# Scaling rows inside the transposing product: a diagonal matrix in place of pre-scaled rows and an identity transpose

## The chip, the cores and the metric

The kernel runs on one core of one Trainium2 chip. The metric is the device time of one launch in microseconds, as the median over several runs. Weights are streamed from HBM, all activations stay on the chip.

## The reference

The reference is a small hybrid transformer on 256 tokens of `x` and 256 tokens of context, width 1024, float32. It has an even layer (RWKV7 recurrence and window attention), a wide squared-ReLU feed-forward block, an odd layer (neighbourhood attention and global attention), a second feed-forward block, a third layer (sparse attention and retention) and a gated feed-forward block, and a last norm. What the change touches is the root-mean-square norm in front of every block:

```python
def rms_norm(x, g):
    xf = x.astype(jnp.float32)
    y = xf * lax.rsqrt(jnp.mean(xf * xf, axis=-1, keepdims=True) + NORM_EPS)
    return (y * g.astype(jnp.float32)).astype(x.dtype)

def modulate(h, gain, shift, scale):
    return rms_norm(h, gain) * (1 + scale) + shift
```

## The kernel before

The residual stream `H` lies token-major: tile k holds 128 tokens on the partitions and 1024 features in a row. The projections want the features on the partitions, so the norm of a tile k also turns it. The norm of a tile is the generator `normed(T, k)`, which puts these steps into one common `plan`; each engine then walks the plan in order and issues its own part of each step.

1. `residual` (where there is one): ScalarE takes a root (L2525), VectorE inverts it (L1931) and adds the scaled output of the block before to `H` (L1961).
2. `square`: ScalarE sums the squares of the row (L2514) and takes the root (L2516).
3. `scale rows`: VectorE inverts the root (L1931) and writes features 0 to 511 of the row times the inverse into the buffer `XH` (L1936); ScalarE does features 512 to 1023 (L2520), after it has waited for the inverse.
4. `x`, twice (q = 0 and q = 4): TensorE turns four 128x128 blocks of the scaled rows into one PSUM bank with `transpose` (L1477). The q = 0 wait is for VectorE's half, the q = 4 wait for ScalarE's half. VectorE applies gain and shift to the q = 0 bank (four instructions, L1948, or L1950 where there is no shift), ScalarE to the q = 4 bank (four instructions, L2538).
5. `x hi`: ScalarE rounds both halves to the fp32r type (L2473). `x lo`: VectorE subtracts to get the rest (L1955). The projections (L1412 to L1414) multiply such pairs in three products and wait for `x lo`.

There are 18 such tile norms: four each before the even layer (T = m0), the first feed-forward block (f0) and the odd layer (m1), two each before the second feed-forward block (f1), the third layer (m2) and the last feed-forward block (u). For f0, m1, f1 and m2 the steps are woven into the output projection that comes before: of the tiles of that projection, tile m is finished (L2551 squares it on ScalarE, L1972, L1975 or L1978 gate it on VectorE), and then the norm of tile m starts; the `x` step of a tile comes between or behind later products of the projection in TensorE's order. In f1 and m2 the order on ScalarE is: L2551 of tile 1, gain and shift of tile 0 (L2538), root for the residual of tile 1 (L2525), rounding of tile 0, squares of tile 1. In m0 and u the tiles follow each other without a projection between them.

`spread` makes a row vector into a 128x1024 tile: the vector stands on the partitions, is read as a broadcast 128x128 block, and is turned by TensorE (L1485), four blocks for each half; ScalarE copies out the first half, VectorE the second (L1926). There are 8 spreads, 64 transposed blocks: two for each of two gates, one for each of two more gates, one for the retention norm and one for the last norm.

Operands of the transposes and of these products are float32. `split_product` of the large projections works on fp32r views instead.

Of the kernel before, what the change touches and what calls it, by code (L numbers as in the profile page):

```python
def program(nc, I, C, out):
# [8 lines left out]
    ACT = mybir.ActivationFunctionType  # L10
    AX = mybir.AxisListType
    MUL, ADD, SUB, MAX = ALU.mult, ALU.add, ALU.subtract, ALU.max
# [9 lines left out]
    extra = ctx.enter_context(nc.sbuf_tensor("extra", [128, 3584], F32))  # L22
# [73 lines left out]
    pe, ve, sc, gp, sp = Line("tensor_done"), Line("vector_done"), Line("scalar_done"), Line("pool_done"), Line("sync_done")  # L96
    ENG = [pe, ve, sc, gp]
    table = {}

    def at(*key):  # L100
        return table.setdefault(key, Point())
# [16 lines left out]
    def sb(*shape):  # L118
        n = 1
        for x in shape:  # L120
            n *= x
        a = arena[:, top[0]:top[0] + n]
        top[0] += n
        assert top[0] <= AREA, top[0]
        if len(shape) == 2:
            a = a.rearrange("p (a b) -> p a b", a=shape[0])
        elif len(shape) == 3:
            a = a.rearrange("p (a b c) -> p a b c", a=shape[0], b=shape[1])
        return a
# [29 lines left out]
    XT, XH = sb(8, 512), sb(8, 512)  # L159
# [8 lines left out]
    H = sb(4, 1024)  # L168
# [4 lines left out]
    DER = sb(8, 8, 2)  # L173
    SSQ = sb(4, 2)
    RS = sb(4, 4)
    SV = sb(8, 32)
    arow = [sb(256), sb(256)]
    sel = sb(2)
# [2 lines left out]
    ident = sb(128)  # L181
# [7 lines left out]
    def step(*a):  # L189
        plan.append(a)  # L190
# [10 lines left out]
    def take(*key):  # L201
        assert idle, "no bank"
        b, before = idle.pop(0)
        assert key not in uses, key
        uses[key] = Use(b, before)

    def give(*key):
        u = uses[key]
        idle.append((u.b, u.empty))

    def bank(*key):
        return uses[key]
# [148 lines left out]
    def col(name, j=0, n=1):  # L361
        r = place[name][0]
        return VC[:, r + j:r + j + n]
# [27 lines left out]
    norms = {}  # L391
# [7 lines left out]
    def normed(T, k, before=None):  # L399
        if before:  # L400
            step("residual", T, k)
        yield
        step("square", T, k)
        yield
        step("scale rows", T, k)
        yield
        for q in (0, 4):
            take("x", T, k, q)
            step("x", T, k, q)
            give("x", T, k, q)  # L410
        yield
        for q in (0, 4):
            step("x hi", T, k, q)
        yield
        for q in (0, 4):
            step("x lo", T, k, q)
        yield

    def rows_of(k, q):
        return H[:, k, q * 128:q * 128 + 512].rearrange("p (a b) -> p a b", a=4)  # L420

    def scaled_rows(k, q):

        return XH[:, q:q + 4, k * 128:k * 128 + 128]

    def x_ready(T, ks):
        return [at("x lo", T, k, 4) for k in ks]
# [88 lines left out]
    step("root table")  # L516
    norms["m0"] = Norm(*at_x(0), None, [at("h", 0)], [at("gain", 0)])
    tiles = [normed("m0", k) for k in range(4)]
    step("load h", 0)
    for n, _ in enumerate(modulation(0, 0, 8)):  # L520
# [402 lines left out]
    def others():  # L923
        for k in FIRST[:7]:
# [11 lines left out]
    norms["f0"] = Norm(*ff_x(0, 1), "mix0", [at("h", 1), *stage("recurrence")], [at("gain", 1)])  # L936
    out_proj("mix0", [(I["w_out"][0], k, k, 4) for k in (4, 0)], OP, 4, O_e, (), {k: [at("part o", k)] for k in range(8)}, gate=True,
             then=[normed("f0", k, True) for k in range(4)])
    xr = x_ready("f0", range(4))
    step("end", "mix0")  # L940
# [7 lines left out]
    def ffn(i, ntok, xr, T, norm_gain, norm_shift, points):  # L948
# [8 lines left out]
        for part in range(32 // nt):  # L957
# [30 lines left out]
            if end:  # L988
                norms[T] = Norm(norm_gain, norm_shift, ("ff2", i, part), [*stage(("ff1", i, part))])
            out_proj(("ff2", i, part), parts, F.h1, ntok, F.O, (), {j: [at("ff1 part", i, part, j)] for j in range(nt)},  # L990
                     part > 0, end, then=[normed(T, k, True) for k in range(ntok)] if end else ())
        return x_ready(T, range(ntok))

# [221 lines left out]
    for pair in range(4):  # L1215
        g = pair // 2
        for qt in range(2):
            q, n = qN[:, pair, qt * 128:qt * 128 + 128], 128 * (qt + 1)
# [188 lines left out]
    def tensor(e):  # L1407
# [50 lines left out]
        def mod(i, s):  # L1458
            w, u = chunks["mod", i, s], bank("mod", i, s)
            pe.wait_ge(w.landed, u.before, at("sv"))  # L1460
            for k in range(8):
                q = 32 * (k % 4)
                t = e.matmul(u.b[q:q + 32, 0:256], SV[:, k, :], w.v[:, k, :], start=k < 4, stop=k >= 4)  # L1463
            t.then_inc(*pe.tick(u.full, w.used))
# [7 lines left out]

        def norm_x(T, k, q):
            u = bank("x", T, k, q)
            pe.wait_ge(at("scaled rows", T, k, q), u.before)
            for j in range(4):
                t = e.transpose(u.b[:, j * 128:j * 128 + 128], scaled_rows(k, q)[:, j, :], ident)  # L1477
            t.then_inc(*pe.tick(u.full))

        def spread(key, half):  # L1480
            vecs, dst, points = spreads[key]
            u = bank("spread", key, half)
            pe.wait_ge(u.before, *points)
            for j in range(4):
                t = e.transpose(u.b[:, j * 128:j * 128 + 128], vecs(half * 4 + j).to_broadcast([128, 128]), ident)  # L1485
            t.then_inc(*pe.tick(u.full))

        def wide(w, x, x0, m, u, first, stop, *points, last=False):
# [391 lines left out]
    def vector(e):  # L1880
        ve.begin(e)

        def vc(part):
            u = bank("vc", part)
            ve.wait_ge(ve.last(), u.full)
            if part == 0:
                e.tensor_copy(VC[:, 0:128], u.b[:, 0:128]).then_inc(*ve.tick(u.empty, at("vc 0")))
                ve.wait_ge(ve.last())
                e.memset(SV, 0.0).then_inc(*ve.tick(at("sv zero")))
                e.memset(eps, 1e-6).then_inc(*ve.tick())  # L1890
                e.memset(eps_gn, 64e-5).then_inc(*ve.tick(at("eps")))
            else:
                e.tensor_copy(VC[:, 128:row], u.b[:, 128:row]).then_inc(*ve.tick(u.empty, at("vc 1")))
# [34 lines left out]
        def inverse(k, *rooted):  # L1928

            ve.wait_ge(ve.last(), at(*rooted))  # L1930
            e.reciprocal(RS[:, k, 2:3], RS[:, k, 1:2]).then_inc(*ve.tick(at("inv", *rooted)))  # L1931

        def scale_rows(T, k):
            inverse(k, "root", T, k)
            ve.wait_ge(ve.last(), *norms[T].points)
            e.tensor_scalar(scaled_rows(k, 0), rows_of(k, 0), RS[:, k, 2:3], None, MUL).then_inc(*ve.tick(at("scaled rows", T, k, 0)))  # L1936

        def norm_x(T, k, q):
            p, u, s = norms[T], bank("x", T, k, q), 0 if k < 2 else 1
# [17 lines left out]
        def residual(T, k):  # L1957
            p = norms[T]
            inverse(k, "res root", T, k)
            ve.wait_ge(ve.last(), *p.points)  # L1960
            e.scalar_tensor_tensor(out=H[:, k, :], in0=outs[p.of].O[:, k, :], scalar=RS[:, k, 2:3], in1=H[:, k, :], op0=MUL,  # L1961
                                   op1=ADD).then_inc(*ve.tick(at("residual", T, k)))

        def out_block(name, c, m):
            p, u, s = outs[name], bank("out", name, c, m), slice(c * 512, c * 512 + 512)
            o, i, r = p.O[:, m, s], u.b[:, :], GB[:, m // 2, s]
            if p.gate and c:
                ve.wait_ge(ve.last(), at("out square", name, 0, m))
                e.tensor_scalar(RS[:, m, 3:4], SSQ[:, m, 0:1], 1.0 / 1024, 1e-6, MUL, ADD).then_inc(*ve.tick(at("first squares", name, m)))
            if p.add:  # L1970
# [466 lines left out]
        def final(k):  # L2437
# [7 lines left out]
                *ve.tick(at("final", k)))  # L2445

        steps = {"vc 0": lambda: vc(0), "vc 1": lambda: vc(1), "turn": turn, "split": split, "gain": gain, "gate": gate,
                 "spread": spread, "scale rows": scale_rows, "x": norm_x, "x lo": x_lo, "residual": residual, "out block": out_block,
                 "even start": even_start, "qB": qB_, "vB": vB_, "sink": sink, "pA": pA_, "rotate": rotate_, "swap": swap_,
                 "round masks": round_masks, "round caus": round_caus, "scores": scores, "scale p": scale_p, "values": values, "recurrence start": recurrence_start,  # L2450
                 "unit grams": unit_grams, "unit tlt": unit_tlt,
# [16 lines left out]
    def scalar(e):  # L2468
# [20 lines left out]
        def silu():  # L2489
            sc.wait_ge(sc.last(), at("vc 0"), at("sv zero"))  # L2490
            e.activation(SV[:, :, 0], col("c", 0, 8), ACT.Silu).then_inc(*sc.tick())
            sc.wait_ge(sc.last())
            e.activation(SV[:, :, 1], col("c_ctx", 0, 8), ACT.Silu).then_inc(*sc.tick(at("sv")))

# [16 lines left out]
        def square(T, k):  # L2511
            p = norms[T]
            sc.wait_ge(sc.last(), *([at("residual", T, k)] if p.of else []), *p.points)
            e.activation(JUNK, H[:, k, :], ACT.Square, accum_out=RS[:, k, 0:1]).then_inc(*sc.tick(at("squared", T, k)))  # L2514
            sc.wait_ge(sc.last(), at("eps"))
            e.activation(RS[:, k, 1:2], RS[:, k, 0:1], ACT.Sqrt, scale=1.0 / 1024, bias=eps).then_inc(*sc.tick(at("root", T, k)))  # L2516

        def scale_rows(T, k):
            sc.wait_ge(sc.last(), at("inv", "root", T, k), *norms[T].points)
            e.activation(scaled_rows(k, 4), rows_of(k, 4), ACT.Identity, scale=RS[:, k, 2:3]).then_inc(*sc.tick(at("scaled rows", T, k, 4)))  # L2520

        def residual(T, k):
            p = norms[T]
# [312 lines left out]
        def final(k):  # L2836
# [4 lines left out]
            e.activation(tiny[:, 4 * k + 1:4 * k + 2], a, ACT.Sqrt, scale=1.0 / 1024, bias=eps).then_inc(*sc.tick(at("final root", k)))  # L2841

        steps = {"load h": load_h, "more columns": more_columns, "silu": silu, "mod": mod, "split": split, "spread": spread,
                 "square": square, "root table": root_table, "scale rows": scale_rows, "x": norm_x, "x hi": x_hi,
                 "residual": residual, "out block": out_block,
                 "even start": even_start, "kB": kB_, "vB": vB_, "pA": pA_, "pA gates": pA_gates, "scores": scores, "turn p": turn_p,
                 "unit grams": unit_grams, "unit lt": unit_lt, "unit turned": unit_turned, "unit lv": unit_lv, "unit solve": unit_solve,
# [125 lines left out]
    block = ctx.enter_context(nc.Block())  # L2973
# [107 lines left out]
```

## Time and profile before

| | us |
|---|---|
| median of 3 runs | 2058.72 (2058.27 to 2063.38) |
| the profiled execution | 2063.38 |
| its span, first to last instruction | 2061.6 |
| TensorE matmul busy | 1844.8 (89%) |
| TensorE weight load busy | 1537.0 (75%) |
| VectorE busy | 1100.0 (53%) |
| ScalarE busy | 904.6 (44%) |
| GpSimd busy | 216.2 (10%) |

The mean granted TensorE clock is 0.943 of full speed. Most of the time TensorE is fed without a gap; where blocks meet, it waits for VectorE and ScalarE. The profiled execution was the slowest of the three runs shown.

### The profile page before, as it was taken

The numbers are of one execution on the slowest core, as the hardware profiler recorded it, in microseconds if no ns is written. First come the engines' busy times: TensorE is split into PE (matmuls) and PEld (weight loads), VectorE is DVE, ScalarE is ACT, GpSimd is POOL, SyncE is SP. The second block draws the span as 40 slices with busy tenths as digits, with TensorE's granted clock in tenths as the row PEclk, the third lists the DMA queues.
The fourth block names the chain that finished last, engine by engine and source line by source line (L and its number), as shares of the span: only waits on it lengthen the run. The fifth ranks groups of instructions, "written<-read, shape, count | busy, mean of one in ns | idle before, by whom it ended". The sixth has DMA issues, their size and how long they took to land.

```text
span 2061.6 us, 39782 instructions
## 1 busy us (share of the span) xinstructions
PE 1844.8 (89%) x16802; PEld 1537.0 (75%) x16802; DVE 1100.0 (53%) x1671; ACT 904.6 (44%) x1448; POOL 216.2 (10%) x214
## 2 busy tenths in 40 slices
PE   5899879899888889999996999799979999679997
PEld 3777658778777778888886776698877677569985
DVE  1457565465555554324435766565445674556863
ACT  3326545344332353223325356565342465346652
POOL 0000034425253000000000200010000000000210
PEclk9999889999998989999998999899989999789998
DMA  8332233222231222333233420355544434245543
GB/s 272 94 123 90 91 112 105 85 84 84 84 105 64 82 82 82 102 102 93 91 102 72 124 81 28 107 182 187 192 131 155 152 103 139 72 132 164 184 156 110
DMA packets 201375, 237.16 MB, mean 115 GB/s; under 512 B 14347, under 2 KB 158573, under 8 KB 201197
## 3 DMA queue, kind: packets, MB, share of 16 engines
q1 hardware_dynamic: 195856, 227.33, 34.7%
q10 hardware_dynamic: 5341, 7.30, 1.0%
q8 instruction: 132, 2.16, 0.4%
q14 instruction: 46, 0.38, 0.1%
HBM read 233.56 MB, written 1.05 MB: 114 GB/s over the span
## 4 chain that ended last, share of the span: by engine, by line
PE 75%; DVE 11%; ACT 7%; issue 2%; POOL 2%; DMA 1%; SPq 1%; ACTq 1%; DVEq 0%; POOLq 0%
PE bank L1412 18%; PE bank L1413 17%; PE bank L1414 17%; PE bank L1604 9%; ACT window L2473 2%; DVE window L1906 2%; PE bank L1592 2%; PE bank L1571 2%; PE bank L1583 2%; PE bank L1463 1%; PE bank L1611 1%; SPq L2934 1%; PE bank L1789 1%; ACT arena L2538 1%; PE bank L1575 1%
## 5 line engine op out<-in xcount | busy, mean ns | idle before, releaser
L1412 PE MATMUL bank<-window 128*128 128x512 f32 (+1 forms) x2152 | 768.6, 357 | 64.8 <-DVE window L1955 27.8
L1413 PE MATMUL bank<-window 128*128 128x512 f32 (+1 forms) x2152 | 754.1, 350 | 0.0
L1414 PE MATMUL bank<-window 128*128 128x512 f32 (+1 forms) x2152 | 753.8, 350 | 0.0
L1412 PEld LDWEIGHTS bank<-window 128*128 128x128 f32 x2152 | 419.6, 195 | 131.1 <-DVE window L1906 32.4
L1906 DVE TENSOR_TENSOR window<-arena,window 128x2048 fp32r<-128x2048 f32 (+1 forms) x164 | 371.4, 2265 | 272.3 <-ACT window L2473 270.4
L2473 ACT ACTIVATE window<-arena 128x2048 fp32r<-128x2048 f32 (+3 forms) x292 | 377.1, 1291 | 198.3 <-PE bank L1414 121.4
L1414 PEld LDWEIGHTS bank<-window 128*128 128x128 f32 x2152 | 419.0, 195 | 50.9
L1413 PEld LDWEIGHTS bank<-window 128*128 128x128 f32 x2152 | 420.2, 195 | 48.1 <-issue 0.2
L2473 ACT ACTIVATE arena<-bank 128x256 f32<-128x256 f32 (+1 forms) x298 | 127.0, 426 | 370.7 <-PE bank L1414 134.9
L1604 PE MATMUL bank<-arena 64*64 64x64 f32 (+1 forms) x5888 | 218.1, 230 | 18.9 <-DVE arena L1398 10.5
L1604 PEld LDWEIGHTS bank<-arena 64*64 64x64 f32 x5888 | 204.8, 139 | 35.4 <-DVE arena L1398 12.2
L2880 POOL TENSOR_TENSOR arena<-arena 128x256 f32<-128x256 f32 x80 | 67.8, 848 | 409.1 <-ACT arena L2473 303.1
L2695 ACT ACTIVATE arena<-bank 128x512 f32<-128x512 f32 (+1 forms) x64 | 31.4, 491 | 142.0 <-PE bank L1414 140.7
L2108 DVE TENSOR_TENSOR arena<-arena,bank 128x512 f32<-128x512 f32 (+1 forms) x80 | 50.7, 634 | 64.7 <-PE bank L1604 63.7
L2597 ACT ACTIVATE arena<-bank,arena 128x512 f32<-128x512 f32 (+3 forms) x112 | 58.5, 522 | 55.0 <-DVE arena L2052 34.0
L2241 DVE TENSOR_TENSOR arena<-arena 128x512 f32<-128x512 f32 (+1 forms) x48 | 29.0, 603 | 78.8 <-ACT arena L2695 78.3
L1463 PE MATMUL bank<-arena 128*32 128x256 f32 x768 | 58.3, 426 | 13.3 <-DMA arena<-in_w_ada 13.1
L2052 DVE TENSOR_REDUCE arena<-bank 128x1 f32<-128x512 f32 (+4 forms) x96 | 51.7, 538 | 22.9 <-PE bank L1575 17.0
L2902 POOL TENSOR_TENSOR arena<-arena 128x2048 f32<-128x2048 f32 x2 | 11.1, 5560 | 483.1 <-DMA arena<-in_c_rpb 483.1
L2473 ACT ACTIVATE extra<-bank 128x512 f32<-128x512 f32 (+2 forms) x96 | 46.9, 489 | 19.4 <-PE bank L1583 16.8
L1470 PEld LDWEIGHTS bank<-arena 128*128 128x128 f32 x192 | 29.0, 213 | 25.5 <-ACT arena L2473 12.1
L1477 PE MATMUL bank<-arena 128*128 128x128 f32 x144 | 26.2, 347 | 23.8 <-DVE arena L1936 23.3
(286 smaller groups left out, 1668.1 us busy)
## 6 DMA issues: line engine op xcount, KB each, us to landing
arena<-in_w_ff SPq DMA_DIRECT2D x64, 1024.0 KB, 5.3
arena<-in_w_ada SPq DMA_DIRECT2D x48, 1024.0 KB, 5.7
arena<-in_w_in SPq DMA_DIRECT2D x23, 1024.0 KB, 5.1
arena<-in_w_ffn_up SPq DMA_DIRECT2D x22, 1024.0 KB, 5.1
arena<-in_w_ffn_down SPq DMA_DIRECT2D x10, 1024.0 KB, 5.1
arena<-in_w_in_even SPq DMA_DIRECT2D x9, 1024.0 KB, 5.5
arena<-in_w_out SPq DMA_DIRECT2D x8, 1024.0 KB, 5.1
arena<-in_w_in_odd SPq DMA_DIRECT2D x8, 1024.0 KB, 5.3
```

The source lines that it names most:

```text
L1412: e.matmul(o, rr(l[0]), rr(r[0]), start=start, stop=False)
L1413: e.matmul(o, rr(l[0]), rr(r[1]), start=False, stop=False)
L1414: return e.matmul(o, rr(l[1]), rr(r[0]), start=False, stop=stop)
L1463: t = e.matmul(u.b[q:q + 32, 0:256], SV[:, k, :], w.v[:, k, :], start=k < 4, stop=k >= 4)
L1571: t = e.matmul(b if it["ns"] > 1 else b[:, 0], it["q"][h0:h1], k, start=True, stop=not it["masks"])
L1604: t = e.matmul(o[h0:h1, c], l[i][h0:h1, c], r[i][h0:h1, c], start=i == 0, stop=i == len(l) - 1)
L1906: e.tensor_tensor(rr(raw), raw, rr(w.high, F32), SUB).then_inc(*ve.tick(w.ready))
L2052: e.tensor_reduce(low[:, h * ns:h * ns + ns], b, AX.X, MAX, negate=True).then_inc(*ve.tick(at("max", S, i, h)))
L2108: e.tensor_tensor(w, w, x, SUB).then_inc(*ve.tick(b.empty, at("w", *u)))
L2473: return e.activation(o, i, ACT.Copy, **k)
L2597: e.activation(a.P[i % a.NP][h][:, s * n:s * n + n], u.b[:, s * n:s * n + n], ACT.Exp, bias=low[:, x:x + 1], accum_out=total[:, x:x + 1]). ...
L2880: return e.tensor_tensor(z.L[l % 2], z.G[:, :, 0], lvl[:, 1 - d, l:l + 1, :].to_broadcast([128, NCH, 64]), MUL)
```

## The change

The step `scale rows` becomes a step `diag`: VectorE inverts the root as before and then writes the identity matrix times the inverse, a 128x128 diagonal matrix, into a part of the buffer `extra` that nothing else uses in those stretches. ScalarE has no part in it. TensorE's `x` step multiplies each 128x128 block of the raw `H` with that diagonal matrix by a plain `matmul` in float32 in place of `transpose`; scale and turn come out of one product. Both halves wait only for `diag`. In `spread` the call `transpose` becomes a plain `matmul` with the identity.

```diff
+    DIAG = extra[:, 2048:2560].rearrange("p (a b) -> p a b", a=4)
...
-        step("scale rows", T, k)
+        step("diag", T, k)
...
-    def rows_of(k, q):
-        return H[:, k, q * 128:q * 128 + 512].rearrange("p (a b) -> p a b", a=4)
-
-    def scaled_rows(k, q):
-
-        return XH[:, q:q + 4, k * 128:k * 128 + 128]
...
         def norm_x(T, k, q):
             u = bank("x", T, k, q)
-            pe.wait_ge(at("scaled rows", T, k, q), u.before)
+            pe.wait_ge(at("diag", T, k), u.before)
             for j in range(4):
-                t = e.transpose(u.b[:, j * 128:j * 128 + 128], scaled_rows(k, q)[:, j, :], ident)
+                t = e.matmul(u.b[:, j * 128:j * 128 + 128], H[:, k, (q + j) * 128:(q + j) * 128 + 128], DIAG[:, k, :],
+                             start=True, stop=True)
             t.then_inc(*pe.tick(u.full))
...
             for j in range(4):
-                t = e.transpose(u.b[:, j * 128:j * 128 + 128], vecs(half * 4 + j).to_broadcast([128, 128]), ident)
+                t = e.matmul(u.b[:, j * 128:j * 128 + 128], vecs(half * 4 + j).to_broadcast([128, 128]), ident, start=True, stop=True)
...
-        def scale_rows(T, k):
+        def diag(T, k):
             inverse(k, "root", T, k)
             ve.wait_ge(ve.last(), *norms[T].points)
-            e.tensor_scalar(scaled_rows(k, 0), rows_of(k, 0), RS[:, k, 2:3], None, MUL).then_inc(*ve.tick(at("scaled rows", T, k, 0)))
+            e.tensor_scalar(DIAG[:, k, :], ident, RS[:, k, 2:3], None, MUL).then_inc(*ve.tick(at("diag", T, k)))
...
-        def scale_rows(T, k):
-            sc.wait_ge(sc.last(), at("inv", "root", T, k), *norms[T].points)
-            e.activation(scaled_rows(k, 4), rows_of(k, 4), ACT.Identity, scale=RS[:, k, 2:3]).then_inc(*sc.tick(at("scaled rows", T, k, 4)))
```

## Rows read from the trace of the kernel before

**Rows 1.** The page, part 4: shares of the chain that ended last.
```profile
PE 75%; DVE 11%; ACT 7%; issue 2%; POOL 2%; DMA 1%; SPq 1%; ACTq 1%; DVEq 0%; POOLq 0%
```

**Rows 2.** Groups by shape, TensorE: shapes xcount | busy us, mean ns | idle before.
```profile
L1470 PE MATMUL bank<-arena 128*128 128x2 f32 x192 | 31.8, 270 | 10.4 <-ACT arena L2473 10.4
L1477 PE MATMUL bank<-arena 128*128 128x128 f32 x144 | 26.2, 347 | 23.8 <-DVE arena L1936 23.3 <-ACT arena L2520 0.4
```

**Rows 3.** Timeline, TensorE: start us, us from first start to last end.
```profile
1747.41 0.38 PE L1823 MATMUL bank<-arena 128*128 128x128 f32 x2
...
767.40 1.91 PE L1485 MATMUL bank<-arena 128*128 128x128 f32 x16
```

**Rows 4.** Single lines: min/median/max ns, first to last start; the last row is the timeline's.
```profile
L1485 PE MATMUL bank<-arena x64: 270/272/473, 650.8 to 2048.6; 128*128 128x128 f32 x64
...
L1936 DVE TENSOR_SCALAR arena<-arena x18: 485/486/490, 33.6 to 1844.7; 128x512 f32<-128x512 f32 x18
L2520 ACT ACTIVATE arena<-arena x18: 721/722/727, 37.9 to 1845.2; 128x512 f32<-128x512 f32 x18
...
1086.36 0.15 DVE L1969 TENSOR_SCALAR arena<-arena 128x1 f32<-128x1 f32 x1
```

**Rows 5.** Timeline of f0, ScalarE, VectorE and TensorE.
```profile
719.79 0.73 ACT L2520 ACTIVATE arena<-arena 128x512 f32<-128x512 f32 x1 [0.36 <-DVE arena L1931]
720.55 1.44 ACT L2538 ACTIVATE arena<-bank,arena 128x128 f32<-128x128 f32 x3
...
722.52 1.30 ACT L2473 ACTIVATE window<-arena 128x512 fp32r<-128x512 f32 x2
...
720.25 1.75 DVE L1948 TENSOR_SCALAR arena<-bank,arena 128x128 f32<-128x128 f32 x4
...
740.04 0.72 ACT L2520 ACTIVATE arena<-arena 128x512 f32<-128x512 f32 x1 [0.36 <-DVE arena L1931]
...
750.45 1.06 PE L1477 MATMUL bank<-arena 128*128 128x128 f32 x8
```

**Rows 6.** Timeline of m1, ScalarE, norm of tile 3.
```profile
1115.75 0.72 ACT L2520 ACTIVATE arena<-arena 128x512 f32<-128x512 f32 x1 [0.36 <-DVE arena L1931]
```

**Rows 7.** Timeline of f1, TensorE, ScalarE and VectorE.
```profile
1302.55 1.09 PE L1477 MATMUL bank<-arena 128*128 128x128 f32 x8
1310.01 1.97 PE L1477 MATMUL bank<-arena 128*128 128x128 f32 x8 [6.37 <-DVE arena L1936]
...
1302.82 0.60 ACT L2551 ACTIVATE extra<-bank 128x512 f32<-128x512 f32 x1
...
1303.74 1.93 ACT L2538 ACTIVATE arena<-bank,arena 128x128 f32<-128x128 f32 x4 [0.23 <-PE bank L1477]
...
1306.12 0.16 DVE L1931 RECIPROCAL arena<-arena 128x1 f32<-128x1 f32 x1
```

**Rows 8.** Timeline of m2, ScalarE.
```profile
1501.17 1.57 ACT L2538 ACTIVATE arena<-bank,arena 128x128 f32<-128x128 f32 x4 [0.24 <-PE bank L1477]
```

**Rows 9.** Timeline of u, TensorE and ScalarE.
```profile
1845.17 2.82 PE L1477 MATMUL bank<-arena 128*128 128x128 f32 x12 [0.36 <-ACT arena L2520]
...
1846.39 3.27 ACT L2538 ACTIVATE arena<-bank,arena 128x128 f32<-128x128 f32 x8 [0.51 <-PE bank L1477]
```

**Rows 10.** Timeline of m0, all engines.
```profile
48.99 6.21 PE L1477 MATMUL bank<-arena 128*128 128x128 f32 x32
...
50.99 3.89 ACT L2538 ACTIVATE arena<-bank,arena 128x128 f32<-128x128 f32 x8 [3.56 <-PE bank L1477]
...
60.68 0.58 PE L1412 MATMUL bank<-window 128*128 128x256 f32 x1 [5.48 <-DVE window L1955]
```

**Rows 11.** Windows of f1: length, busy of PE, PEld, DVE, ACT, POOL; granted clock; DMA.
```profile
1316.00:1318.00 2.00, 1.75 (x8) 1.76 (x9) 0.99 (x3) 1.27 (x1) 0.00 (x0) 0.50 0.00 0
...
1320.00:1322.00 2.00, 2.00 (x17) 2.00 (x16) 0.18 (x1) 0.38 (x1) 0.00 (x0) 0.87 0.00 0
```

**Rows 12.** The chain in order of time, a spread inside the recurrence.
```profile
665.18 1.04 PE bank L1485 x4
```

More of the change, by code:

```diff
@@ L2447, in vector @@
         steps = {"vc 0": lambda: vc(0), "vc 1": lambda: vc(1), "turn": turn, "split": split, "gain": gain, "gate": gate,
-                 "spread": spread, "scale rows": scale_rows, "x": norm_x, "x lo": x_lo, "residual": residual, "out block": out_block,
+                 "spread": spread, "diag": diag, "x": norm_x, "x lo": x_lo, "residual": residual, "out block": out_block,
                  "even start": even_start, "qB": qB_, "vB": vB_, "sink": sink, "pA": pA_, "rotate": rotate_, "swap": swap_,
@@ L2843, in scalar @@
         steps = {"load h": load_h, "more columns": more_columns, "silu": silu, "mod": mod, "split": split, "spread": spread,
-                 "square": square, "root table": root_table, "scale rows": scale_rows, "x": norm_x, "x hi": x_hi,
+                 "square": square, "root table": root_table, "x": norm_x, "x hi": x_hi,
                  "residual": residual, "out block": out_block,
```

## The prediction

> **What bounds the kernel.** I read the chain that ended last first. TensorE holds three quarters of it, VectorE and ScalarE together 18% [rows 1]: long runs of products, and joints where a norm runs on VectorE and ScalarE. The edit sits at the joints, so I took the groups by shape for the counts, then the chain and the timeline of each engine around all six norms. What the reader should see is that work of the norm is on the path in some places (a row of TensorE that waits for L1936) and beside other work elsewhere.
>
> **Price of the new product.** The 96 plain float32 products of the modulation turn (48 turns, two each) are 192 records; the 144 transposes of the norms (18 tiles of eight) are 144 records, and those of the spreads (eight of eight) are 64 [rows 2, 4]. So a plain float32 product is issued as two load and multiply records, a transpose as one. Sixteen transposes take 1.91 us; less the length of one (0.27) that is 1.64/15 = 0.11 us apiece. A plain product of the same shape, L1823, takes 0.38 for its two records, and again (0.38 - 0.27) = 0.11 lies between them [rows 3, 4]. Hence one extra record of 0.11 us for each of the 208 blocks at full clock. At half clock eight transposes take 1.97, (1.97 - 0.42 - small gaps)/7 = 0.213 apiece [rows 7]. One tile costs 0.88 us more on TensorE at full clock and 1.7 at half clock, a half spread 0.44 or 0.85.
>
> The Trainium skill, page "TensorE: Matmul & The Clock Gate", section Terms, has a transpose mode that is four times faster for FP32. By that each block would gain three records' time and not one; the rows of L1823 speak for one. I keep it as a rival.
>
> **Price of what goes.** VectorE's 128x512 multiply takes 0.486 us, ScalarE's 0.722 [rows 4]. The new 128x128 multiply does not stand in the trace: it is bounded by 0.15 (one column) and 0.486 (512 columns) [rows 4]; a line between them gives 0.15 + 0.336/4 = 0.23, so VectorE saves 0.25 a tile (0 to 0.34). ScalarE saves its 0.72 and the 0.36 for which it stood waiting on the inverse.
>
> **f0.** ScalarE's L2520 at 719.79 stands in front of gain and shift of the tile before, 720.55, already turned. Without it these start at 719.45, 1.1 earlier. But rounding, at 722.52, also needs VectorE's four L1948, which end at 722.00 and come only 0.25 earlier, at 721.75; with the handover rounding starts at 721.8, so 0.7 is won and not 1.1 [rows 5]. The same happens a tile later (0.7). After the scale of the last tile, 740.04, ScalarE goes straight on to rounding a weight chunk for which TensorE waits: 1.1 won in full. TensorE's extra 0.88 for tiles 0 and 1 falls where it is some 2.7 us ahead of ScalarE, and for tile 2 in a wait; it costs nothing there. If that cover were gone it would be 0.9 each. The turn of tile 3, at 750.45, is on the chain: +0.9 [rows 5]. Sum -0.7 - 0.7 - 1.1 + 0.9 = -1.6.
>
> **m1.** The same pattern, with the last scale at 1115.75 in front of five DMA issues and a chunk's rounding, all of which move up [rows 6], and VectorE's 0.25 once more, since the gate of tile 1 follows L1936 directly: -1.9.
>
> **f1.** Here nothing is ahead. L2551 at 1302.82 can't move up: TensorE reaches the turn at 1302.55 straight out of the product that L2551 reads, whose tail ends about 1302.7. The q = 4 bank is full after 16 records instead of 8, 0.9 later; ScalarE already waits for it (0.23 idle) and starts gain and shift at 1304.6 instead of 1303.74. They end at 1306.5, and the root L2525 for the residual of tile 1 is queued behind them and ends at 1306.9, so VectorE's inverse comes at 1306.95 instead of 1306.12: +0.8. Then the residual, squares and root follow unchanged; VectorE's diagonal is 0.25 faster; TensorE's turn of tile 1 at 1310.01 is on the path at half clock: +1.7 [rows 7]. Sum +2.3.
>
> **m2.** As f1, but gain and shift take 1.57 and not 1.93 [rows 8], so the delay of the inverse is 0.7: +0.7 - 0.25 + 1.7 = +2.1.
>
> **u.** Sixteen transposes at half clock, the last twelve from 1845.17, are read by eight ScalarE instructions from 1846.39 to 1849.66 [rows 9]. New: the first diagonal is 0.25 earlier and nothing waits for ScalarE, so 32 records run from 1843.45 and end at 1843.45 + 31 x 0.213 + 0.42 = 1850.5. The second four of ScalarE start then, not at 1848.1, and end at 1852.1: +2.4 with half clock throughout. If the clock rises on the way, up to 1.0 comes back. I take +1.9.
>
> **m0.** The scales are done by 41 us, in a wait for a weight DMA: nothing is won. The 32 transposes last 6.21 us, which is 24 gaps of 0.213 and 7 of 0.11: the clock rises near 54.2. ScalarE's reading starts after eight records and runs without a gap until the projection starts at 60.68 [rows 10]. New: ScalarE's first bank is full at 48.99 + 15 x 0.213 + 0.42 = 52.6, its second at 55.2, where it would have been free at 54.7; the rest follows at its own pace. Sum +2.2 (1.5 with an earlier rise).
>
> **Spreads.** The one at 665.18 is on the chain at half clock: +0.85 [rows 12]. Sixteen records at 767.40 in the gapless run of the feed-forward block [rows 3]: +1.75. The pair before the odd gate +0.44, the one in the second feed-forward block +0.88, the last norm's +0.88. Those at 650.8 and 1739.7 lie in waits of TensorE: 0 (0.44 and 0.88 if the cover goes). Sum +4.8.
>
> No DMA, no SP or GpSimd instruction moves except the five issues in m1. No new wait is made; the q = 4 turn waits for VectorE where it waited for ScalarE.
>
> **Total.** -1.6 - 1.9 + 2.3 + 2.1 + 1.9 + 2.2 + 4.8 = +9.8 us, 0.48%. On the profiled execution, 2063.38, that gives 2073.2. That execution was 4.7 above the median, so for the median I add the same to 2058.72: 2068.5.
>
> **Rivals.**
> *The clock gives it back.* In f1 TensorE idles 6.37 us before the turn, its records there have the half-clock spacing [rows 7], and the projection that starts at 1316.25 still runs at 0.50 until about 1320.3 [rows 11]. With twice the records in the turn, the clock could be up when the projections start in m0, f1, m2 and u; with four slow starts like this one of 4 us, half of 16, 8, would come back: +2, 2060.6. For it: m0's clock did rise during the turn [rows 10]. Against: afterwards TensorE still idles about 4 us in each place, and in m0 it was down again after such a pause. The Trainium skill, the same page, Part 4: PE-mode transpose, says that transposes do not count as busy for the clock; by it plain products would help here more than m0 lets one expect. Chance 0.19.
>
> *Only the relief counts.* If the second record of a block cost nothing (the pair done inside the 0.11 of one), the place that decides is the turn itself; from under 0.03 us for an extra record the sum changes sign. Then f0 and m1 give -2.5 and -2.75, f1 and m2 -0.3 each, u -0.9, in all -6.8: 2051.9. Against it stands L1823. Chance 0.08.
>
> *Three extra records per block.* The TensorE terms of the path triple: the positive parts of f0 and m1 become 5.3, f1 and m2 5.2 + 1.6 each, u and m0 about 8 each, spreads 14.4, relief -6.8: about +43, 2101. Chance 0.05.
>
> **Numbers.** My forecast has 0.68, its own range +5 to +15 (2063.7 to 2073.7): below, if the cover is better or the clock rises earlier; above, if the two hidden spreads, tiles 0 to 2 of f0 and m1 and the cold readings of u all count (0.4 + 0.9 + 5.3 + 0.5 = 7, of which I take most). The range for 8 in 10 reaches down to the clock rival and leaves out the other two: 2059.5 to 2075.5. A measurement here tells about 0.3%, 6.2 us, from no change. Slower by more: 0.62 of my forecast's 0.68 and the last rival's 0.05, 0.67; within: the clock rival and the low end of mine, 0.25; faster 0.08.
>
> **What would show it.** L1477 with 288 records and L1485 with 128, 0.11 apart; VectorE's diagonal at about 0.23 us; ScalarE's L2520 gone and gain and shift of f0 right behind the root; in f1 and m2 a longer wait of ScalarE for the turn of tile 0, and about 3.6 us for the turn of tile 1; the projection of u starting about 11 us after the root of tile 1 instead of 9. The prediction is wrong if the extra records are not 0.11 apart, if the clock is up at the start of the projections, or if in f0 TensorE turns out not to be ahead.

## The result and the profile after

The changed kernel takes 2073.48 us in the median (2071.06 to 2074.85, 4 runs) against 2060.22 (2058.27 to 2063.38, 4 runs) for the kernel before on the same chip. The ratio of the runs is 1.0057, with a 95% interval from 1.0040 to 1.0076: 0.57% slower, about 11.7 us. The two medians themselves lie 13.3 us apart; here and below, a difference in us that stands beside a ratio is worked out from the ratio. The forecast was 0.48% slower, 9.8 us. Its time, 2068.5, was 5 us low; 1.5 of these come from before's own median, which was 2060.22 in these runs and not 2058.72. The profiled executions have spans of 2061.6 and 2070.3, 8.7 apart.

The chain that ended last, and the two groups of the norms' turn, from the page and the groups of the changed kernel (shares by engine; line, shapes xcount | busy us, mean ns | idle before):

```profile
PE 75%; DVE 11%; ACT 6%; issue 2%; POOL 2%; DMA 1%; SPq 1%; ACTq 1%; DVEq 0%; POOLq 0%
...
L1471 PE MATMUL bank<-extra,arena 128*128 128x128 f32 x288 | 43.0, 316 | 17.7 <-DVE extra L1931 17.7
L1471 PEld LDWEIGHTS bank<-extra,arena 128*128 128x128 f32 x288 | 41.7, 230 | 19.7 <-DVE extra L1931 19.2
```

Single lines of the changed kernel (min/median/max ns), the spreads' product and the new diagonal:

```profile
L1480 PE MATMUL bank<-arena x128: 270/275/580, 652.0 to 2057.3; 128*128 128x128 f32 x128
...
L1931 DVE TENSOR_SCALAR extra<-arena x18: 285/286/289, 33.9 to 1851.0; 128x128 f32<-128x128 f32 x18
```

The counts are 288 and 128 where they were 144 and 64 [rows 2, 4]: one more record per block, as forecast. TensorE's wait for VectorE before the turn went from 23.3 [rows 2] to 17.7 us. The diagonal takes 0.286 us.

Timeline of f0 in the changed kernel, to be held against [rows 5]:

```profile
718.76 1.93 ACT L2529 ACTIVATE arena<-bank,arena 128x128 f32<-128x128 f32 x4
721.20 1.30 ACT L2468 ACTIVATE window<-arena 128x512 fp32r<-128x512 f32 x2 [0.50 <-DVE arena L1943]
...
719.35 1.75 DVE L1943 TENSOR_SCALAR arena<-bank,arena 128x128 f32<-128x128 f32 x4
...
737.79 3.85 ACT L2468 ACTIVATE window<-arena 128x2048 fp32r<-128x2048 f32 x2
...
747.43 2.37 PE L1471 MATMUL bank<-extra,arena 128*128 128x128 f32 x16
```

Gain and shift on ScalarE start right behind the root, and then ScalarE waits 0.50 us for VectorE before it can round: the 1.1 us shrink to 0.6, close to the 0.7 of the prediction and for its reason.

Timeline of f1 in the changed kernel, to be held against [rows 7]:

```profile
1302.91 1.95 PE L1471 MATMUL bank<-extra,arena 128*128 128x128 f32 x16
1311.00 3.79 PE L1471 MATMUL bank<-extra,arena 128*128 128x128 f32 x16 [6.15 <-DVE extra L1931]
1319.05 0.58 PE L1406 MATMUL bank<-window 128*128 128x256 f32 x1 [4.26 <-DVE window L1950]
...
1303.16 0.60 ACT L2542 ACTIVATE extra<-bank 128x512 f32<-128x512 f32 x1 [1.29 <-PE bank L1408]
...
1304.95 1.93 ACT L2529 ACTIVATE arena<-bank,arena 128x128 f32<-128x128 f32 x4 [1.10 <-PE bank L1471]
1306.91 0.29 ACT L2516 ACTIVATE arena<-arena 128x1 f32<-128x1 f32 x1
...
1307.31 0.16 DVE L1926 RECIPROCAL arena<-arena 128x1 f32<-128x1 f32 x1 [0.88 <-ACT arena L2516]
```

The squares of tile 1's projection (L2542) now show a wait for TensorE, but start no later: 0.25 us behind the start of the turn, 0.27 before. The turn of tile 0 makes ScalarE wait 1.10 us instead of 0.23, the root L2516 queues behind gain and shift, and VectorE, which had no wait there, waits 0.88. The second turn takes 3.79 us instead of 1.97.

Windows of f1 in the changed kernel (length, busy of PE, PEld, DVE, ACT, POOL; granted clock; DMA), against [rows 11]:

```profile
1314.00:1316.00 2.00, 0.79 (x4) 0.49 (x3) 0.86 (x3) 1.05 (x3) 0.00 (x0) 0.77 0.00 0
1316.00:1318.00 2.00, 0.00 (x0) 0.00 (x0) 0.43 (x1) 1.90 (x4) 0.00 (x0) 1.00 0.00 0
1318.00:1320.00 2.00, 0.95 (x4) 0.96 (x5) 1.13 (x3) 1.97 (x2) 0.00 (x0) 0.58 0.00 0
1320.00:1322.00 2.00, 2.00 (x12) 2.00 (x11) 1.82 (x1) 0.07 (x1) 0.00 (x0) 0.50 0.00 0
...
1324.00:1326.00 2.00, 2.00 (x14) 2.00 (x14) 0.42 (x1) 0.38 (x1) 0.00 (x0) 0.71 0.00 0
```

The clock rises at the end of the turn, is up while TensorE idles, and is down again when the projection starts at 1319.05. The projection then runs slowly to about 1325.2, some 6 us, where it was 4 before.

For the other norms I take one stretch each from both traces, from the first row of squares of tile 0 (in m0 from the first turned record) to the first product of the block behind it that needs the last tile's norm (in m0 that of the projection's first half). In us:

| | before | changed | measured | forecast |
|---|---|---|---|---|
| m0 | 48.99 to 60.68 | 49.28 to 62.05 | +1.1 | +2.2 |
| f0 | 712.11 to 755.78 | 711.77 to 754.07 | -1.4 | -1.6 |
| m1 | 1084.06 to 1135.19 | 1084.20 to 1134.05 | -1.3 | -1.9 |
| f1 | 1300.23 to 1316.24 | 1300.39 to 1319.05 | +2.7 | +2.3 |
| m2 | 1497.66 to 1513.07 | 1502.18 to 1519.83 | +2.2 | +2.1 |
| u | 1841.38 to 1853.35 | 1847.69 to 1860.62 | +1.0 | +1.9 |
| sum | | | +4.3 | +5.0 |

### The profile page after: what moved, and what is told of

Same layout as the page of the kernel before. It is cut to its first block, busy times and chain, and to the rows that moved or that the text cites. A ratio compares the mean times of both kernels' runs of the same rounds, so it can differ in the third digit from the quotient of the medians.

```text
span 2070.3 us, 40165 instructions
## 1 busy us (share of the span) xinstructions
PE 1856.4 (90%) x17010; PEld 1554.2 (75%) x17010; DVE 1098.3 (53%) x1671; ACT 891.6 (43%) x1430; POOL 216.5 (10%) x214
## 4 chain that ended last, share of the span: by engine, by line
PE 75%; DVE 11%; ACT 6%; issue 2%; POOL 2%; DMA 1%; SPq 1%; ACTq 1%; DVEq 0%; POOLq 0%
PE bank L1406 18%; PE bank L1407 17%; PE bank L1408 17%; PE bank L1599 9%; ACT window L2468 2%; DVE window L1901 2%; PE bank L1587 2%; PE bank L1566 2%; PE bank L1578 2%; PE bank L1457 1%; PE bank L1471 1%; SPq L2925 1%; PE bank L1606 1%; PE bank L1784 1%; DVE window L1950 1%
## 5 line engine op out<-in xcount | busy, mean ns | idle before, releaser
L1599 PEld LDWEIGHTS bank<-arena 64*64 64x64 f32 x5888 | 201.8, 137 | 35.9 <-issue 12.2
L2893 POOL TENSOR_TENSOR arena<-arena 128x2048 f32<-128x2048 f32 x2 | 11.1, 5568 | 480.5 <-DMA arena<-in_c_rpb 480.4
L1471 PE MATMUL bank<-extra,arena 128*128 128x128 f32 x288 | 43.0, 316 | 17.7 <-DVE extra L1931 17.7
L1471 PEld LDWEIGHTS bank<-extra,arena 128*128 128x128 f32 x288 | 41.7, 230 | 19.7 <-DVE extra L1931 19.2
```

The costliest lines, as they stand in the source:

```text
L1471: t = e.matmul(u.b[:, j * 128:j * 128 + 128], H[:, k, (q + j) * 128:(q + j) * 128 + 128], DIAG[:, k, :], start=True, stop=True)
L1599: t = e.matmul(o[h0:h1, c], l[i][h0:h1, c], r[i][h0:h1, c], start=i == 0, stop=i == len(l) - 1)
```

## The experiments

Ratios are to the kernel before, whose runs on the same chip had medians of 2059.6, 2059.4 and 2062.5 us in the three groups of four.

**The spreads alone.**

```diff
-                t = e.transpose(u.b[:, j * 128:j * 128 + 128], vecs(half * 4 + j).to_broadcast([128, 128]), ident)
+                t = e.matmul(u.b[:, j * 128:j * 128 + 128], vecs(half * 4 + j).to_broadcast([128, 128]), ident, start=True, stop=True)
```

> Kernel before with only the spreads changed to plain products. Theory A (each plain 128x128 product is one record of 0.11 us more, and it counts where TensorE is on the chain): +4.8 us, ratio 1.0023. Rival B (TensorE's added records lie beside other work, and what the changed kernel lost is the moment at which the clock rises and falls): within 1 us of before, ratio 1.000. Rival C (a record costs more than 0.11 us there): over +8 us.

Measured: 1.0023 (1.0011 to 1.0036), 2064.17 us, +4.7. Theory A: B's 1.000 lies below the interval, and C's +8 us is a ratio of 1.0039, above it. Two sites can be read from the traces, by the start of the same instructions in both kernels: the changed kernel loses 1.8 us at the spread of 767 and 0.9 at that of the last norm, this kernel 1.9 and 1.0; the forecast had 1.75 and 0.88. The row of the spreads in its trace:

```profile
L1485 PE MATMUL bank<-arena x128: 270/275/580, 647.2 to 2049.0; 128*128 128x128 f32 x128
```

**The norms alone.** The changed kernel with the line above turned back.

> Changed kernel with transposes again in the spreads; norms by the diagonal product. Theory A: relief and cost of the norms sum to +5.0 us, ratio 1.0024, and this plus the spread run gives the whole change, +9.8. Rival B: the whole of the change's 11.8 us stays here, ratio 1.0057. Rival D (the relief outweighs, the spreads alone are the loss): below before, ratio 0.999 or less.

Measured: 1.0042 (1.0026 to 1.0059), 2069.84 us over 5 runs, +8.7 (5.4 to 12.2). D falls. B's 1.0057 lies inside this interval; what speaks against B is the run before, in which the spreads alone cost 4.7 us. A's 1.0024 lies just below the interval. The sum with the spreads is +13.4, and the whole change is 8.2 to 15.7, so the two parts add up within their scatter; the norms cost more than the 5.0 that the forecast gave them.

**Relief without the second record.**

```diff
-                t = e.matmul(u.b[:, j * 128:j * 128 + 128], H[:, k, (q + j) * 128:(q + j) * 128 + 128], DIAG[:, k, :],
-                             start=True, stop=True)
+                t = e.transpose(u.b[:, j * 128:j * 128 + 128], H[:, k, (q + j) * 128:(q + j) * 128 + 128], ident)
```

> As the changed kernel, with the diagonal matrix still made and waited for, but the blocks of the raw rows turned by a transpose, so that the scaling by the inverse root is left out of the result; transposes in the spreads. It has the relief of VectorE and ScalarE without the second record. Theory A: f0 -2.5, m1 -2.75, f1 and m2 -0.3 each, u -0.9, in all -6.8 us, ratio 0.9967. Rival E (ScalarE's scale was hidden, VectorE waits for TensorE anyway): within 1.5 us of before.

This kernel leaves the scale out of its result and serves for timing alone. Measured: 0.9965 (0.9951 to 0.9980), 2053.79 us, -7.2. Theory A. In its trace the norm of u, from the squares at 1830.15 to the end of the last `x lo` at 1841.24, takes 11.1 us against 11.9 before. The turn of f1 is back at its old length and ScalarE's wait at 0.26:

```profile
1294.51 1.10 PE L1471 MATMUL bank<-arena 128*128 128x128 f32 x8
1301.77 1.97 PE L1471 MATMUL bank<-arena 128*128 128x128 f32 x8 [6.16 <-DVE extra L1930]
...
1295.71 1.93 ACT L2528 ACTIVATE arena<-bank,arena 128x128 f32<-128x128 f32 x4 [0.26 <-PE bank L1471]
```

**Cost without the relief.**

```diff
-                t = e.transpose(u.b[:, j * 128:j * 128 + 128], scaled_rows(k, q)[:, j, :], ident)
+                t = e.matmul(u.b[:, j * 128:j * 128 + 128], scaled_rows(k, q)[:, j, :], ident, start=True, stop=True)
```

> Kernel before with the rows still scaled by VectorE and ScalarE, and each block of them turned by a plain product with the identity instead of a transpose; spreads as before. Theory A: the cost of the norms alone, m0 +2.2, f0 and m1 +0.9 each, f1 +2.5, m2 +2.4, u +2.6, in all about +11.5 us, ratio 1.0056. Rival B (hidden): under +3 us. With the relief run it should add up to the norm run: -6.8 and +11.5 give +4.7.

Measured: 1.0063 (1.0046 to 1.0079), 2073.97 us over 6 runs, +13.0. Theory A. With the relief's -7.2 this makes +5.8. Its f1 shows the cost with the old scaling in place:

```profile
1302.51 2.05 PE L1477 MATMUL bank<-arena 128*128 128x128 f32 x16
1310.91 3.42 PE L1477 MATMUL bank<-arena 128*128 128x128 f32 x16 [6.35 <-DVE arena L1936]
...
1304.66 1.93 ACT L2538 ACTIVATE arena<-bank,arena 128x128 f32<-128x128 f32 x4 [1.19 <-PE bank L1477]
```

**The diagonal product at some norms only.** Five kernels are the kernel before with one condition that says which tile norms go by the diagonal product; the spreads stay transposes.

```diff
+    def by_diag(T, k):
+        return T in ("f0", "m1")
...
+                if by_diag(T, k):
+                    t = e.matmul(o, H[:, k, (q + j) * 128:(q + j) * 128 + 128], DIAG[:, k, :], start=True, stop=True)
+                else:
+                    t = e.transpose(o, scaled_rows(k, q)[:, j, :], ident)
...
++            o, i = (DIAG[:, k, :], ident) if by_diag(T, k) else (scaled_rows(k, 0), rows_of(k, 0))
+            e.tensor_scalar(o, i, RS[:, k, 2:3], None, MUL).then_inc(*ve.tick(at("scaled rows", T, k, 0)))
...
+            if by_diag(T, k):
+                return
             sc.wait_ge(sc.last(), at("inv", "root", T, k), *norms[T].points)
```

> Kernel before, with the diagonal product in the eight tile norms of f0 and m1 only. Theory A (where ScalarE's scale stood in front of other work and TensorE is ahead, the change wins): the prediction's -3.5 us, ratio 0.9983; by the trace of the changed kernel, where f0 and m1 won 1.0 and 1.5, -2.5, ratio 0.9988. Rival F (the norms lose wherever they are put): above 1.001.

Measured: 0.9990 (0.9978 to 1.0001), 2057.51 us, -2.1. F's loss is excluded, and both of A's numbers lie inside; the sign is A's, though no change at all is just inside the interval. In its trace the stretches of the table take 41.4 us in f0 and 48.9 in m1, against 43.7 and 51.1.

> Kernel before, with the diagonal product in the four tile norms of f1 and m2 only. Theory A: +4.4 us by the prediction, +4.9 by the trace of the changed kernel, ratio 1.0021 to 1.0024. Rival F (the loss is spread evenly over the 18 tiles, 5.0 x 4/18): +1.1, ratio 1.0005.

Measured: 1.0026 (1.0014 to 1.0039), 2066.04 us, +5.4. Theory A; the even spread of F is below the interval. The four tiles of f1 and m2, 4 of 18, lose far more than an even share.

> Kernel before, with the diagonal product in the six tile norms of m0 and u only. Theory A at half clock throughout: +4.1 us, ratio 1.0020. If the clock rises during the longer turn, as the trace of the changed kernel shows it: +1.35 and +0.96, ratio 1.0011.

Measured: 1.0045 (1.0031 to 1.0060), 2068.65 us over 6 runs, +9.3. Neither expectation: too much by a factor of two. In its trace the norm of u, 1842.48 to 1856.61, takes 14.1 us, +2.2: half clock until the last few records. That is more than in the changed kernel's trace, but leaves some 5 us unexplained. So I ran the two halves and the pair again.

> Kernel before, with the diagonal product in the four tile norms of m0 only. m0 and u together came out at 1.0045, though in that run's trace m0 itself was 0.8 to 1.1 us longer and u 2.2. Theory A (local cost): +1.1 us, ratio 1.0005. Rival H (the later start of what follows m0 moves TensorE's clock in the recurrence and costs there): 1.002 or more, with the squares of f0 more than 3 us later than before's.

Measured: 1.0021 (1.0009 to 1.0032), 2066.57 us, +4.3. A's 1.0005 lies below the interval (1.9 to 6.6 us). H asked for 1.002 or more and for squares of f0 more than 3 us later; they start at 715.52 instead of 712.11, so both hold by number. But H's reason, the clock in the recurrence, is not shown: 2.7 of these 3.4 us are there by 100 us already, and traces of kernels that share the old m0 scatter by more (below). Here the turn took 9.75 us and not 8.63, since the clock rose later, and the projection's slow start came after it. That start lasts about 5.0 us at half clock instead of 3.7, which costs some 0.6 more on top of the 2.0 of the stretch:

```profile
49.10 9.75 PE L1483 MATMUL bank<-extra,arena 128*128 128x128 f32 x64
62.82 0.58 PE L1416 MATMUL bank<-window 128*128 128x256 f32 x1 [3.98 <-DVE window L1964]
```

> Kernel before, with the diagonal product in the two tile norms of u only. Theory A: +2.2 us at half clock, ratio 1.0011. Rival H (something behind u is hit as well): 1.002 or more.

Measured: 1.0006 (0.9989 to 1.0022), 2063.67 us, +1.2. This is nearer to A's 1.0011, but H's 1.002 lies inside the interval too; the run does not decide. The rows of u:

```profile
1835.88 6.69 PE L1483 MATMUL bank<-extra,arena 128*128 128x128 f32 x32 [3.08 <-DVE extra L1945]
1847.93 0.58 PE L1416 MATMUL bank<-window 128*128 128x256 f32 x1 [5.35 <-DVE window L1964]
```

Thirty-two records in 6.69 us, all but the last few at half clock (the clock rose near 1841.9), and the projection 14.2 us after the squares at 1833.77, +2.2.

> The kernel of the m0 and u run once more, on the same chip as its two halves. Theory A: +3.3 us, ratio 1.0016, the sum of the halves; then the 1.0045 of the first time was the scatter of the clock over six runs. Rival H: 1.0045 again.

Measured: 1.0035 (1.0021 to 1.0049), 2070.00 us, +7.2. The expected 1.0016 is excluded; the two halves add up to 1.0027, which is not. H's 1.0045 lies inside as well. Taken with the first run of this kernel, m0 and u together cost 7.2 to 9.3 us, where the forecast's terms for them are 4.1; how that is shared between m0 and u these runs do not settle.

**The same relief without the product.** ScalarE's part of the scaling is given to engines that idle at that moment.

```diff
+    def by_pool(T, k, q):
+        return T in ("f0", "m1") and (q == 4 or k != 2)
...
+        def scale_rows(T, k):
+            for q in (0, 4):
+                if by_pool(T, k, q):
+                    gp.wait_ge(gp.last(), at("inv", "root", T, k), *norms[T].points)
+                    e.tensor_scalar(scaled_rows(k, q), rows_of(k, q), RS[:, k, 2:3], None, MUL).then_inc(
+                        *gp.tick(at("scaled rows", T, k, q)))
```

> Kernel before (transposes everywhere), but in f0 and m1 GpSimd scales the second half of each row instead of ScalarE, and for tiles 0, 1 and 3 the first half instead of VectorE too. It has the relief of ScalarE and VectorE and no second record. Theory A: 1.0 for each of the two tiles that stand in front of gain and shift and 1.1 for the last, in f0 and in m1: -6.2 us, ratio 0.9970. Rival G (GpSimd's multiply is too slow, about 1.7 us a half, and TensorE waits for it in its place, or it slows VectorE): at or above 0.9995.

Measured: 0.9983 (0.9968 to 0.9997), 2055.31 us, -3.5. Faster. The interval holds A's 0.9970 and, just, G's 0.9995. By the trace f0 shortens from 43.7 to 40.4 us and m1 does not (51.4 against 51.1), so the relief is whole in one place and lost in the other. In m1 the five DMA issues behind the block's end wait for all engines, GpSimd's multiplies of tile 3 among them, and ScalarE's rounding of the chunk waits behind these issues:

```profile
1109.35 3.22 POOL L2910 TENSOR_SCALAR arena<-arena 128x512 f32<-128x512 f32 x2 [10.43 <-DVE arena L1934]
...
1112.68 0.35 ACTq L2492 DMA_DIRECT2D arena<-t_Rax  x1
...
1115.48 1.91 ACT L2478 ACTIVATE window<-arena 128x2048 fp32r<-128x2048 f32 x1 [6.56 <-issue]
```

The next version keeps GpSimd for tiles 0 to 2 and lets VectorE scale both halves of tile 3:

```diff
+        return T in ("f0", "m1") and k < 3
...
             e.tensor_scalar(scaled_rows(k, 0), rows_of(k, 0), RS[:, k, 2:3], None, MUL).then_inc(*ve.tick(at("scaled rows", T, k, 0)))
+            if T in ("f0", "m1"):
+                e.tensor_scalar(scaled_rows(k, 4), rows_of(k, 4), RS[:, k, 2:3], None, MUL).then_inc(*ve.tick(at("scaled rows", T, k, 4)))
```

> Kernel before (transposes everywhere), but in f0 and m1 GpSimd scales both halves of the rows of tiles 0 to 2, and VectorE both halves of tile 3, where VectorE is idle; so that no DMA issue waits for GpSimd. Theory A: 1.0 + 1.0 + 1.1 us in f0, the same and a little more in m1, -6.2 us, ratio 0.9970. Rival G (GpSimd's two multiplies take 3.2 us, and TensorE's turn of tile 2 comes too late): 0.999 or more.

Measured: 0.9963 (0.9946 to 0.9979), 2056.28 us, -7.6. Theory A; G's 0.999 is excluded. The kernel beats both others. In its trace f0 takes 39.5 us and m1 48.1, 4.2 and 3.1 less than before, which together is near the 7.6 of the timed runs. The issues in m1 now start 1.2 us after the root ends at 1104.37, instead of 3.8, and VectorE's two multiplies of 0.49 end at 1105.55:

```profile
1104.66 0.49 DVE L1941 TENSOR_SCALAR arena<-arena 128x512 f32<-128x512 f32 x1
1105.07 0.48 DVE L1943 TENSOR_SCALAR arena<-arena 128x512 f32<-128x512 f32 x1
...
1105.58 0.35 ACTq L2494 DMA_DIRECT2D arena<-t_Rax  x1
```

## Why the prediction was right, and where it was off

**The price of the product** held. One record more per block, 16 records in 1.95 us at full clock, (1.95 - 0.27)/15 = 0.11 apart. The rival of three extra records does not show in this kernel's rows: 288 records for 144 blocks, factor two. The Trainium skill ("TensorE: Matmul & The Clock Gate", Terms) calls transpose mode four times faster for FP32; the traces here show about twice, eight blocks in 1.04 us as transposes (at 717.32 in the trace before) and in 1.95 as products.

**The price of the diagonal** was put at 0.23 and is 0.286; the line between a one-column and a 512-column row was too low. It costs 0.05 us per tile.

**f0 and m1.** TensorE was ahead, as supposed, and the reliefs are there, a little smaller: 0.6 for each of the two tiles and not 0.7, since rounding waits for VectorE, whose diagonal is slower than forecast. Up to the `x lo` of tile 2 m1 takes 29.8 us in the changed kernel against 31.2, of which 0.2 is the earlier gate; the relief run and the norms run show the same 29.8. The end of m1 won less than forecast, and for this the rows give a cause. The five DMA issues were put 1.1 us earlier, the length of ScalarE's scale and its wait. But they wait for the end of the block on all engines, so now for VectorE's diagonal. Before:

```profile
1116.56 0.35 ACTq L2487 DMA_DIRECT2D arena<-t_Rax  x1
```

In the changed kernel:

```profile
1113.82 0.29 ACT L2511 ACTIVATE arena<-arena 128x1 f32<-128x1 f32 x1
...
1114.41 0.28 DVE L1931 TENSOR_SCALAR extra<-arena 128x128 f32<-128x128 f32 x1
...
1114.73 0.35 ACTq L2482 DMA_DIRECT2D arena<-t_Rax  x1
```

The issues start 0.6 us behind the root's end where it was 1.2, so 0.6 is won and not 1.1. With 1.4 won before and 0.8 lost at the last turn this gives the 1.3 of the table. Beyond that the stretch of m1 scatters: it takes 48.9 us in the run with f0 and m1 and 50.5 in the norms run, with the same code in it.

**f1 and m2** held to 0.4 us in the stretches of the table, and the run with these two alone gives +5.4 for the forecast 4.4. The stretches end at the first product; f1's slow start behind it is 2 us longer, which costs about 1 more, while m2's ends 3.3 us behind the first product instead of 5.4, which gives about 1 back. The wait that moved, TensorE before ScalarE before the root before VectorE's inverse, is in the rows above.

**The spreads** were +4.8 by forecast and +4.7 (2.3 to 7.4) by their own run.

**m0 and u.** For u the forecast took a value between half clock throughout and a clock that rises on the way. Both occur: 5.46 us for the 32 records in the changed kernel, 6.69 in the run with u alone. The first is the exception: five of the six traces with the plain product in u have +2.2 or +2.3 for the stretch, the changed kernel's alone +1.0. For m0 the stretch to the projection became longer by 1.1 in the changed kernel and by about 2.0 in the run with m0 alone (49.10 to 62.82, 13.7 against 11.7); there the clock rises near 54.2, as in the trace before, and the forecast 2.2 fits, while in the changed kernel it rises near 52. What the prediction did not ask is whether the shift costs something behind m0. The kernels with the old m0 start the squares of f0 between 705.7 and 717.1 us, their mean over seven traces is 709.7; the six with the plain product in m0 start between 711.8 and 718.1, mean 714.2. That is +4.5, of which the norm itself has 1 to 2. It would fit the +4.3 of m0 alone. But it is not shown that such a cost exists, nor how it would arise: among the seven that do not differ there the start scatters by 11 us, and 4.5 between means of seven and six is not far outside such scatter.

**The clock rival** (0.19) was right in that the mean granted clock rose, from 0.943 to 0.955, and wrong in what this gives. In f1 the gain lies in the turn and in the idle time behind it, and the slow start of the projection grew; m2's shrank by as much. In f0 and m1 the clock is indeed up when the first half of the projection starts (its first row takes 0.39 us at 732.02, against 0.58 at 733.96 before), but TensorE then waits for a weight chunk all the same (4.12 and 9.10 us, against 3.93 and 7.89). What the clock gave elsewhere I did not isolate. The relief rival (0.08) is refuted by L1471's own records, and the relief run measured its size: forecast -6.8, measured -7.2.

**The total.** Of the 8.7 us between the two spans the stretches of the table have 4.3, and what lies between them 4.4, next to the forecast's 4.8 for the spreads. That closeness is luck in part. By the starts and ends in the table, the changed kernel gains 1.7 us from m0 to f0, where a spread was to cost 0.85, and loses 1.9 from f0 to m1, 1.3 from m1 to f1 and 1.7 from f1 to m2. The timed runs say 11.7, with an interval that begins at 8.2, so the forecast 9.8 is inside. The term that came out too small is that of m0 and u together, 4.1 by forecast and 7.2 and 9.3 in two runs whose intervals both begin above it; its rest of some 3 us or more stays open. The parts do not close either: -2.1 for f0 and m1, +5.4 for f1 and m2 and 7.2 to 9.3 for m0 and u make 10.5 to 12.6, where the norms in one kernel cost 8.7 (5.4 to 12.2).

## What to carry to other kernels

Folding a scale into a transposing product looks like saving a pass over the rows, but in float32 it trades one record per block for two on the engine that carries three quarters of the chain. Price such an edit site by site: the same edit won 0.6 us where ScalarE's multiply stood in front of work that was ready, and lost 2.2 to 2.7 us where the turn itself was next. And where an in-order engine does something early that nobody needs yet, give it to an engine that idles there; but look which later waits ask for that engine's end.

## What the runs showed that I had not expected

The scatter of one and the same kernel goes with the clock. Of 29 runs of the kernel before in the second group of four, the fastest (2051.98 us) had a mean granted clock of 0.949 and the slowest (2068.51) one of 0.940; over all 29 the correlation of time and clock is -0.94. By these two clocks the half-clock time is about 209 and 248 us, an estimate, and 39 us more at half clock can cost up to 20; 16.5 are seen. An edit of 10 us is of the size of that scatter, and two traces can differ by 10 us in a stretch of code that is the same in both.

GpSimd scaled two halves of 128x512 in 3.22 us nearly every time (nine of twelve pairs in the two GpSimd kernels), while VectorE's instructions beside it kept their lengths to 0.04 us: four gains and shifts 1.75 us, the residual 1.28 to 1.32. Two pairs took 3.73, and one took 5.34, beside the splits of weight chunks on VectorE:

```profile
737.38 5.34 POOL L2910 TENSOR_SCALAR arena<-arena 128x512 f32<-128x512 f32 x2 [8.82 <-DVE arena L1934]
...
737.45 0.64 DVE L1921 TENSOR_TENSOR arena<-arena 128x16 f32<-128x16 f32 x1
738.99 4.99 DVE L1909 TENSOR_TENSOR window<-arena,window 128x2048 fp32r<-128x2048 f32 x2 [0.91 <-ACT window L2478]
```

There VectorE paid too: the two splits take 4.62 us in the kernel before, and the 128x16 instruction 0.18. So the 3.22 us did not hold in every place; one such pair shows no more than that.
